# Attention with the values as one high|low tile in two passes, and row sums on GpSimd

## The chip, the cores and the metric

The kernel runs on one core of a Trainium2 chip. The core has a matrix engine (TensorE, PE in the rows; its weight loads are PEld), a vector engine (VectorE, DVE), an activation engine (ScalarE, ACT), GpSimd (POOL) and a queue engine that here only issues transfers (SyncE, SP). They run their own instruction streams and meet at semaphores. The metric is the device time of one execution in microseconds, lower is better.

## The reference

One layer of a hybrid decoder, for a sequence of 2048 tokens of width 1024: a normalised input, one input projection, three token mixers side by side (a recurrent block, forgetting attention, gated linear attention), an output projection and a gated feed-forward. The change is in the forgetting attention, 6 heads of width 64:

```
q = rms_norm(q, q_gain); k = rms_norm(k, k_gain)
cum = cumsum(log_sigmoid(f_logit + b_f))
s = einsum('qd,kd->qk', q, k) * scale + cum[:, None] - cum[None, :]
s = where(k_pos <= q_pos, s, -inf)
p = softmax(s)
o = einsum('qk,kd->qd', p, v)
```

Everything is in 32-bit floats. The kernel gets near that precision by splitting an operand in a high part, rounded to the reduced matmul type (F32R), and a low part, the rest, and adding up the products of the parts.

## The kernel before

The kernel is a row of stages: input projection with the recurrent block, preparation of the attention operands (`fox_operands`), `forgetting_attention`, the gated linear attention, output projection, feed-forward. Each stage is a block with one program for each engine, and stages don't overlap.

`forgetting_attention` makes a loop of 3 passes (`LOOPS`), each over 2 heads. A head has 4 blocks of 512 queries; a block of one head is a unit, 8 units in a pass. A unit is worked off in items: an item is one tile of 128 keys (`kt`) against the unit's 512 queries, so block b has 4(b+1) items and a pass has 80. In the last four items of a unit, the diagonal ones, only 512, 384, 256 and 128 queries are left by the causal mask.

Scores are made twice. `score` makes chunks with queries on partitions (`fa_s_ps`, lines L903 to L906), from which DVE takes row maxima (`maxima`, L850), 22 chunks ahead of their use; `turn_m` and ACT's `copy_m` bring the negated maxima into the operands. `score_t` makes the transposed scores of an item, keys on partitions (`fa_st_ps`, L931 to L934), maxima already subtracted, 3 items ahead (`AHEAD`), in `TB` = 3 PSUM banks: item m+3 takes the bank of item m.

For every item ACT takes the exponential twice, as f32 (`fa_probs`, L822) and rounded (`fa_p_hi`, L823). The residual `fa_p_lo` = `fa_probs` - `fa_p_hi` is made by POOL (L786) for items with kt % 3 = 1, 78 of the 240, and by DVE (L878) for the others. All three have `PB` = 4 buffers, which the value product frees (`pv_done`). PE then makes the value product in three passes (`times_v`):

```
nc.tensor.matmul(o_ps[:, u % 2, qs], v[:, hh, kt, 0:VW], p_hi[:, m % PB, qs], start=first, stop=False, skip_group_check=True)
nc.tensor.matmul(o_ps[0:HEAD_DIM, u % 2, qs], v[:, hh, kt, VW:VW + HEAD_DIM], p_hi[:, m % PB, qs], start=False, stop=False, skip_group_check=True)
nc.tensor.matmul(o_ps[:, u % 2, qs], v[:, hh, kt, 0:VW], p_lo[:, m % PB, qs], start=False, stop=end, skip_group_check=True).then_inc(pv_done, 1)
```

The stationary operand `v[..., 0:VW]` holds the high part of the values in 64 columns and ones in the other 64, so the lower half of `fa_o_ps` is the output and its upper half the row sum. The second pass has the low part of the values, 64 columns.

PE's program is in this order for each item m: score chunk m+22, transposed scores m+3, `turn_m` where one is due, value product m. At the end of a unit its sum is inverted: at kt = 3 of the next unit ACT takes Ln and Exp (`invert`, L815 and L817, each with a table load), DVE waits in `correct` (kt = 2, L865) and makes one Newton step and the scaling in `finish` (kt = 3, L870 and L874); then ACT issues the store. The order of the work is that of the programs; nothing plans it. POOL also copies the values of the next heads into `fa_v` in two pieces (`place_v`, L775 and L776).

Of the kernel before, what the change touches and what calls it, by code (L numbers as in the profile page):

```python
# [14 lines left out]
F32 = mybir.dt.float32  # L15
F32R = mybir.dt.float32r
# [5 lines left out]
P = 128  # L22
# [59 lines left out]
def project_in_and_recur(nc, vec, mod, xT, w_mod, w_in, w_gates, consts, vec_in, proj, mix):  # L82
# [14 lines left out]
    with ExitStack() as ctx:  # L97
        sb = lambda n, s, d=F32: ctx.enter_context(nc.sbuf_tensor(n, s, d))
        ps = lambda n, s, d=F32: ctx.enter_context(nc.psum_tensor(n, s, d))
        sem = lambda n: ctx.enter_context(nc.semaphore(n))  # L100
# [395 lines left out]

def fox_operands(nc, vec, consts, fox_rows, proj, q_split, k_split, bias_split, v_nat):
# [177 lines left out]
def forgetting_attention(nc, consts, q_split, k_split, bias_split, v_nat, mix):  # L675
# [28 lines left out]
    SB, TB, PB = 2, 3, 4  # L704
# [5 lines left out]
    with ExitStack() as ctx:  # L710
# [5 lines left out]
        v = sb("fa_v", [P, HPB, SEQ // P, 3 * HEAD_DIM], F32R)  # L716
# [14 lines left out]
        o_ps, m_ps = ps("fa_o_ps", [P, 2, BLK]), ps("fa_m_ps", [P, BLK])  # L731
# [8 lines left out]
        with nc.Block() as block:  # L740
# [20 lines left out]
            def _(pool):  # L761
# [6 lines left out]
                nc.gpsimd.memset(v[:, :, :, HEAD_DIM:VW].rearrange("p h t n -> p (h t) n").bitcast(F32), 1.0).then_inc(filled, 1)  # L768
                pool.wait_ge(filled, 4)

                def place_v(hh, head, used):

                    pool.wait_ge(pv_done, used)
                    src = v_nat[:, head].rearrange("p o t n -> p (o t) n")
                    nc.gpsimd.tensor_copy(v[:, hh, :, 0:HEAD_DIM], src[:, :, 0:HEAD_DIM].bitcast(F32))  # L775
                    nc.gpsimd.tensor_copy(v[:, hh, :, VW:], src[:, :, HEAD_DIM:].bitcast(F32)).then_inc(v_ready, 1)  # L776

                def lows(base, head):
                    for m, (u, kt, r) in enumerate(ITEMS):
# [4 lines left out]
                        if on_pool(m):  # L784
                            pool.wait_ge(hi_done, base + (m + 1))
                            nc.gpsimd.tensor_tensor(p_lo[:, m % PB, r * P:BLK], probs[:, m % PB, r * P:BLK], p_hi[:, m % PB, r * P:BLK].bitcast(F32),  # L786
                                                    ALU.subtract).then_inc(lo_pool, 1)
                place_v(0, slice(0, 1), NI)
                with pool.Fori(0, LOOPS - 1) as j:
                    lows(NI * j, lambda h: bass.ds(HPB * j + h, 1))  # L790
                last = FOX_HEADS - HPB
                lows(NI * (LOOPS - 1), lambda h: slice(last + h, last + h + 1) if h < HPB else None)

            @block.scalar
            def _(act):
                act.sem_inc(m_copied, 1)
                act.wait_ge(filled, 1)
# [9 lines left out]
                with act.Fori(0, LOOPS) as j:  # L807
# [4 lines left out]
                    def invert(u):  # L812
                        act.wait_ge(pv_done, NI * j + (NI + items_of(u)[-1] + 1))
                        act.wait_ge(fin_done, NU * j + (u + 1))
                        nc.scalar.activation(newton[:, u % 2], o_ps[HEAD_DIM:P, u % 2], ACT.Ln).then_inc(ln_sum, 1)  # L815
                        act.wait_ge(ln_sum, NU * j + (u + 1))
                        nc.scalar.activation(inv_sum[:, u % 2], newton[:, u % 2], ACT.Exp, scale=-1.0).then_inc(inv_done, 1)  # L817
                    for m, (u, kt, r) in enumerate(ITEMS):
                        cols = slice(r * P, BLK)
                        act.wait_ge(st_done, NI * j + (NI + m + 1))  # L820
                        act.wait_ge(pv_done, NI * j + (NI + m + 1 - PB))
                        nc.scalar.activation(probs[:, m % PB, cols], st_ps[:, m % TB, cols], ACT.Exp)  # L822
# [13 lines left out]
            def _(dve):  # L836
# [24 lines left out]
                with dve.Fori(0, LOOPS) as j:  # L861

                    def correct(u):
                        dve.wait_ge(inv_done, NU * j + (u + 1))
                        nc.vector.tensor_tensor(newton[:, u % 2], o_ps[HEAD_DIM:P, u % 2], inv_sum[:, u % 2], ALU.mult).then_inc(corrected, 1)  # L865

                    def finish(u):
                        hh, b = UNITS[u]
                        dve.wait_ge(corrected, 2 * NU * j + (2 * u + 1))
                        nc.vector.scalar_tensor_tensor(out=inv_sum[:, u % 2], in0=newton[:, u % 2], scalar=-2.0, in1=inv_sum[:, u % 2], op0=ALU.add, op1=ALU.mult).then_inc(corrected, 1)  # L870
                        dve.wait_ge(corrected, 2 * NU * j + (2 * u + 2))
# [17 lines left out]
            def _(pe):  # L889
                pe.wait_ge(made, 2)  # L890
                pe.wait_ge(filled, 2)
                pe.sem_inc(st_done, NI)

# [26 lines left out]
                with pe.Fori(0, LOOPS) as j:  # L920
# [16 lines left out]
                    def times_v(m):  # L937
# [17 lines left out]
                    for m in range(NI):  # L955
# [5 lines left out]
                        times_v(m)  # L961
# [775 lines left out]
```

## Time and profile before

| | |
|---|---|
| time, median of 3 runs | 3292.73 us (3290.06 to 3296.04) |
| span of the profiled execution | 3298.2 us |
| PE busy | 2833.0 us, 86% |
| DVE busy | 1457.8 us, 44% |
| ACT busy | 1059.2 us, 32% |
| POOL busy | 900.1 us, 27% |
| attention stage, first score to the start of the next stage | 884 to 1394 us |

No other time is given for the profiled execution than its span; it is 5.5 us above the median of the runs. A busy PE counts overlapping matmuls once and their modelled length, so its share is not its load: the distance between starts is. In a windows row the number behind PE, DVE and so on is its busy time in us, with its instructions in brackets, and the clock is the granted share of full speed. In a timeline row the first number is the start, the second the duration, both in us from the start of the span; what stands in brackets is the idle time of the engine in front of it and what ended that.

### The profile page before, as it was taken

How to read it: one execution, taken by the hardware profiler on the slowest of the kernel's cores; microseconds unless marked ns; L12 is line 12 of the kernel's file. 1: busy time of each engine (PE TensorE's matmuls, PEld its weight loads, DVE VectorE, ACT ScalarE, POOL GpSimd, SP SyncE). 2: the span in 40 equal slices, each digit the busy share in tenths (PEclk: the TensorE clock that was granted, in tenths of full speed). 3: DMA queues.
4: the chain of work that ended last, by engine and by line, in shares of the span. 5: the costliest groups of instructions: out<-in, count | busy, mean ns of one | idle time of the engine just before them, and what ended most of it. 6: DMA issues, size and time to landing. Idle time of an engine off the chain costs nothing. (4 is left out here: it accounts for less than half of the span.)

```text
span 3298.2 us, 34894 instructions
## 1 busy us (share of the span) xinstructions
PE 2833.0 (86%) x12359; PEld 2257.1 (68%) x12359; DVE 1457.8 (44%) x1604; ACT 1059.2 (32%) x1332; POOL 900.1 (27%) x330
## 2 busy tenths in 40 slices
PE   1299999986597979756599699999999999999999
PEld 0177877762275757534487588887888788888887
DVE  5934455525366666555411644314450344214420
ACT  1300134423166666643311233212231222222221
POOL 1301111100121212200132344443444444444343
PEclk9999999996599899956799799999999999999999
DMA  5034333233602020020341422342223322332223
GB/s 218 7 118 169 123 110 93 88 112 105 196 26 66 28 62 0 34 86 13 137 157 76 146 98 92 107 162 96 93 95 132 130 102 88 119 136 90 102 96 102
DMA packets 80770, 330.53 MB, mean 100 GB/s; under 512 B 9239, under 2 KB 10279, under 8 KB 58515
## 3 DMA queue, kind: packets, MB, share of 16 engines
q1 hardware_dynamic: 60368, 280.96, 25.1%
q10 hardware_dynamic: 17984, 39.85, 3.5%
q0 software_dynamic: 2352, 8.93, 0.7%
q8 instruction: 31, 0.51, 0.1%
q14 instruction: 35, 0.28, 0.0%
HBM read 266.69 MB, written 63.01 MB: 100 GB/s over the span
## 5 line engine op out<-in xcount | busy, mean ns | idle before, releaser
L1468 POOL TENSOR_TENSOR ff_w_lo<-ff_w_raw,ff_w_hi 128x2048 fp32r<-128x2048 f32 (+1 forms) x152 | 613.6, 4037 | 879.2 <-ACT ff_w_hi L1497 879.2
L1600 DVE TENSOR_TENSOR ff_a_lo<-ff_gated,ff_a_hi 128x512 f32 x88 | 382.2, 4343 | 148.3 <-ACT ff_a_hi L1507 148.3
L1497 ACT ACTIVATE ff_w_hi<-ff_w_raw 128x2048 fp32r<-128x2048 f32 (+1 forms) x152 | 256.2, 1686 | 356.0 <-PE ff_d_ps L79 356.0
L77 PE MATMUL banks<-h_hi,w_hi 128*128 128x512 f32 x768 | 308.9, 402 | 12.1 <-DVE h_lo L392 12.1
L77 PE MATMUL ff_g_ps<-ff_h_hi,ff_w_hi 128*128 128x512 f32 x704 | 277.5, 394 | 37.8 <-DVE ff_h_lo L1584 31.9
L79 PE MATMUL banks<-h_hi,w_lo 128*128 128x512 f32 x768 | 301.0, 392 | 0.0
L78 PE MATMUL banks<-h_lo,w_hi 128*128 128x512 f32 x768 | 300.9, 392 | 0.0
L78 PE MATMUL ff_g_ps<-ff_h_lo,ff_w_hi 128*128 128x512 f32 x704 | 277.0, 393 | 0.0
L79 PE MATMUL ff_g_ps<-ff_h_hi,ff_w_lo 128*128 128x512 f32 x704 | 276.4, 393 | 0.0
L77 PE MATMUL ff_u_ps<-ff_h_hi,ff_w_hi 128*128 128x512 f32 x704 | 273.9, 389 | 0.0
L78 PE MATMUL ff_u_ps<-ff_h_lo,ff_w_hi 128*128 128x512 f32 x704 | 273.9, 389 | 0.0
L77 PE MATMUL ff_d_ps<-ff_a_hi,ff_w_hi 128*128 128x512 f32 x704 | 273.9, 389 | 0.0
L78 PE MATMUL ff_d_ps<-ff_a_lo,ff_w_hi 128*128 128x512 f32 x704 | 273.9, 389 | 0.0
L79 PE MATMUL ff_d_ps<-ff_a_hi,ff_w_lo 128*128 128x512 f32 x704 | 273.9, 389 | 0.0
L79 PE MATMUL ff_u_ps<-ff_h_hi,ff_w_lo 128*128 128x512 f32 x704 | 273.9, 389 | 0.0
L1503 ACT ACTIVATE ff_silu<-ff_g_ps 128x512 f32<-128x512 f32 x88 | 52.7, 599 | 603.9 <-PE ff_u_ps L79 603.8
L850 DVE TENSOR_REDUCE fa_ch_max<-fa_s_ps 128x1 f32<-128x512 f32 (+2 forms) x262 | 158.9, 607 | 138.3 <-PE fa_s_ps L906 74.9
L1598 DVE TENSOR_TENSOR ff_gated<-ff_silu,ff_u_ps 128x512 f32<-128x512 f32 x88 | 60.5, 688 | 345.8 <-ACT ff_silu L1503 345.8
L786 POOL TENSOR_TENSOR fa_p_lo<-fa_probs,fa_p_hi 128x512 fp32r<-128x512 f32 (+3 forms) x78 | 92.6, 1187 | 404.4 <-ACT fa_p_hi L823 404.4
L1610 DVE SCALAR_TENSOR_TENSOR ff_gated<-ff_d_ps,mod,ff_x_res 128x512 f32<-128x512 f32 x32 | 24.0, 751 | 402.0 <-PE ff_d_ps L79 402.0
L77 PEld LDWEIGHTS ff_g_ps<-ff_h_hi,ff_w_hi 128*128 128x128 f32 x704 | 133.8, 190 | 67.7 <-issue 32.7
L77 PEld LDWEIGHTS banks<-h_hi,w_hi 128*128 128x128 f32 x768 | 145.8, 190 | 45.7 <-DVE h_lo L392 12.5
(253 smaller groups left out, 5208.4 us busy)
## 6 DMA issues: line engine op xcount, KB each, us to landing
ff_w_raw<-in_w_gate_up SPq DMA_DIRECT2D x88, 1024.0 KB, 4.8
ff_w_raw<-in_w_down SPq DMA_DIRECT2D x64, 704.0 KB, 4.0
shared<-in_w_mod SPq DMA_DIRECT2D x24, 1024.0 KB, 6.3
proj_dram<-x_blk SPq DMA_DIRECT2D x96, 256.0 KB, 2.6
w_raw<-in_w_in SPq DMA_DIRECT2D x24, 512.0 KB, 5.1
po_slot<-mix_dram SPq DMA_DIRECT2D x8, 1024.0 KB, 4.8
po_slot<-in_xT SPq DMA_DIRECT2D x8, 1024.0 KB, 4.8
x_dram<-po_slot ACTq DMA_DIRECT2D x8, 1024.0 KB, 3.9
```

What stands on the lines that cost most here:

```text
L77: nc.tensor.matmul(out, hi, act_hi, start=first, stop=False)
L78: nc.tensor.matmul(out, hi, act_lo, start=False, stop=False)
L79: return nc.tensor.matmul(out, lo, act_hi, start=False, stop=last)
L786: nc.gpsimd.tensor_tensor(p_lo[:, m % PB, r * P:BLK], probs[:, m % PB, r * P:BLK], p_hi[:, m % PB, r * P:BLK].bitcast(F32), ALU.subtract). ...
L850: nc.vector.tensor_reduce(ch_max[:, u % 2, i, c:c + 1], s_ps[:, n % SB, 0:w], AX.X, ALU.max).then_inc(max_done, 1)
L1468: nc.gpsimd.tensor_tensor(w_lo[:, s, size(up)], w_raw[:, s, size(up)], w_hi[:, s, size(up)].bitcast(F32), ALU.subtract).then_inc(lo_ready, 1)
L1497: nc.scalar.activation(w_hi[:, s, size(up)], w_raw[:, s, size(up)], ACT.Copy).then_inc(hi_ready, 1)
L1503: nc.scalar.activation(silu[:, s], g_ps[:, s], ACT.Silu).then_inc(silu_ready, 1)
L1598: nc.vector.tensor_tensor(gated[:, s], silu[:, s], u_ps[:, s], ALU.mult).then_inc(gated_ready, 1)
L1600: nc.vector.tensor_tensor(a_lo[:, bass.ds(n, 1)].rearrange("p o n -> p (o n)"), gated[:, s], a_hi[:, bass.ds(n, 1)].rearrange("p o n -> p ...
L1610: nc.vector.scalar_tensor_tensor(out=y_out[:, s], in0=d_ps[:, s], scalar=mod[:, bass.ds(2 * i + (s + GATE2), 1)], in1=x_res[:, s], op0=ALU ...
```

## The change

The stationary operand becomes one tile of 128 columns, high part in 64 and low part in 64, for both passes, over `fa_p_hi` and over `fa_p_lo`. The upper half of `fa_o_ps` is then the product with the low part; DVE copies it out and adds it to the lower half at the end of a unit. The ones are gone from the operand, so the row sums are made elsewhere: for every item POOL adds `fa_probs` into an accumulator `fa_acc` (for kt = 0 it multiplies by a column of ones, which starts the accumulator), and at the end of a unit one f32 matmul with a 128x64 tile of ones adds over the partitions into a new bank, `fa_sum_ps`. ACT now waits also for this addition (`acc_done`) before it writes a buffer of `fa_probs` again. The new bank comes from the transposed scores: `TB` goes from 3 to 2, so item m+3 waits for the exponential of item m+1. The input stage gets a block at its end in which SP clears all of its semaphores (44). The Newton step reads `fa_sum_ps`.

```
@@ project_in_and_recur, behind its block
+        with nc.Block() as block:
+            @block.sync
+            def _(sp):
+                for s in sems:
+                    sp.sem_clear(s)
@@ forgetting_attention
-    SB, TB, PB = 2, 3, 4
+    SB, TB, PB = 2, 2, 4
...
-        v = sb("fa_v", [P, HPB, SEQ // P, 3 * HEAD_DIM], F32R)
+        v = sb("fa_v", [P, HPB, SEQ // P, VW], F32R)
+        acc, ones = sb("fa_acc", [P, 2, BLK]), sb("fa_ones", [P, HEAD_DIM])
...
@@ gpsimd
-                    nc.gpsimd.tensor_copy(v[:, hh, :, 0:HEAD_DIM], src[:, :, 0:HEAD_DIM].bitcast(F32))
-                    nc.gpsimd.tensor_copy(v[:, hh, :, VW:], src[:, :, HEAD_DIM:].bitcast(F32)).then_inc(v_ready, 1)
+                    nc.gpsimd.tensor_copy(v[:, hh], src.bitcast(F32)).then_inc(v_ready, 1)
+                def row_sum(m, base, units):
+                    u, kt, r = ITEMS[m]
+                    pool.wait_ge(hi_done, base + (m + 1))
+                    if kt == 0:
+                        pool.wait_ge(sum_done, units + (u + 1))
+                        nc.gpsimd.tensor_tensor(acc[:, u % 2], probs[:, m % PB], ones[:, 0:1].to_broadcast([P, BLK]), ALU.mult).then_inc(acc_done, 1)
+                    else:
+                        pool.wait_ge(acc_done, base + (m + PB))
+                        nc.gpsimd.tensor_tensor(acc[:, u % 2, r * P:BLK], acc[:, u % 2, r * P:BLK], probs[:, m % PB, r * P:BLK], ALU.add).then_inc(acc_done, 1)
...
+                        row_sum(m, base, units)
@@ scalar
                     def invert(u):
-                        act.wait_ge(pv_done, NI * j + (NI + items_of(u)[-1] + 1))
+                        act.wait_ge(sum_done, NU * j + (u + 3))
...
+                        act.wait_ge(acc_done, NI * j + (m + 1))
                         nc.scalar.activation(probs[:, m % PB, cols], st_ps[:, m % TB, cols], ACT.Exp)
@@ vector, finish
+                        dve.wait_ge(pv_done, NI * j + (NI + items_of(u)[-1] + 1))
+                        dve.wait_ge(corrected, 3 * NU * j + (3 * u + 2))
+                        nc.vector.tensor_copy(newton[:, u % 2], o_ps[HEAD_DIM:P, u % 2]).then_inc(corrected, 1)
+                        dve.wait_ge(corrected, 3 * NU * j + (3 * u + 3))
+                        nc.vector.tensor_tensor(newton[:, u % 2], newton[:, u % 2], o_ps[0:HEAD_DIM, u % 2], ALU.add).then_inc(added, 1)
...
-                        nc.vector.scalar_tensor_tensor(out=o_t[HEAD_DIM * hh:HEAD_DIM * (hh + 1), b], in0=o_ps[0:HEAD_DIM, u % 2], scalar=-1.0, in1=inv_sum[:, u % 2], op0=ALU.mult, op1=ALU.mult).then_inc(fin_done, 1)
+                        nc.vector.scalar_tensor_tensor(out=o_t[HEAD_DIM * hh:HEAD_DIM * (hh + 1), b], in0=newton[:, u % 2], scalar=-1.0, in1=inv_sum[:, u % 2], op0=ALU.mult, op1=ALU.mult).then_inc(fin_done, 1)
@@ tensor
-                        nc.tensor.matmul(o_ps[:, u % 2, qs], v[:, hh, kt, 0:VW], p_hi[:, m % PB, qs], start=first, stop=False, skip_group_check=True)
-                        nc.tensor.matmul(o_ps[0:HEAD_DIM, u % 2, qs], v[:, hh, kt, VW:VW + HEAD_DIM], p_hi[:, m % PB, qs], start=False, stop=False, skip_group_check=True)
-                        nc.tensor.matmul(o_ps[:, u % 2, qs], v[:, hh, kt, 0:VW], p_lo[:, m % PB, qs], start=False, stop=end, skip_group_check=True).then_inc(pv_done, 1)
+                        nc.tensor.matmul(o_ps[:, u % 2, qs], v[:, hh, kt], p_hi[:, m % PB, qs], start=first, stop=False, skip_group_check=True)
+                        nc.tensor.matmul(o_ps[:, u % 2, qs], v[:, hh, kt], p_lo[:, m % PB, qs], start=False, stop=end, skip_group_check=True).then_inc(pv_done, 1)
+                    def row_sums(u):
+                        pe.wait_ge(acc_done, NI * j + (items_of(u)[-1] + 1 + PB))
+                        pe.wait_ge(corrected, 3 * NU * j + 3 * u)
+                        nc.tensor.matmul(sum_ps[0:HEAD_DIM], ones[:], acc[:, u % 2], start=True, stop=True).then_inc(sum_done, 1)
...
                         times_v(m)
+                        if ITEMS[m][0] > 0 and ITEMS[m][1] == 1:
+                            row_sums(ITEMS[m][0] - 1)
+                    row_sums(NU - 1)
```

## Rows read from the trace of the kernel before

**Rows 1.** The page, part 1: busy us, share, instructions.

```profile
PE 2833.0 (86%) x12359; PEld 2257.1 (68%) x12359; DVE 1457.8 (44%) x1604; ACT 1059.2 (32%) x1332; POOL 900.1 (27%) x330
```

**Rows 2.** Windows: item passes, one restart; length, PE, PEld, DVE, ACT, POOL, clock.

```profile
907.00:1057.00 150.00, 135.43 (x653) 107.23 (x654) 99.14 (x177) 106.41 (x198) 35.31 (x30) 0.94 0.11 29
1057.00:1073.00 16.00, 3.70 (x22) 3.10 (x21) 3.83 (x8) 4.29 (x7) 0.00 (x0) 0.64 0.79 198
1073.00:1216.00 143.00, 128.81 (x612) 101.16 (x612) 94.52 (x171) 101.36 (x189) 34.23 (x29) 0.93 0.10 28
...
1234.00:1386.00 152.00, 135.20 (x645) 106.56 (x645) 99.83 (x179) 106.05 (x198) 32.79 (x28) 0.93 0.01 5
```

**Rows 3.** Groups of 884 to 1394 us, shapes apart: busy us, mean ns.

```profile
L878 DVE TENSOR_TENSOR fa_p_lo<-fa_probs,fa_p_hi 128x512 fp32r<-128x512 f32 x114 | 88.7, 778 | 25.6 <-ACT fa_p_hi L823 25.4
...
L950 PE MATMUL fa_o_ps<-fa_p_hi,fa_v 128*64 128x512 f32 x168 | 69.4, 413 | 0.0
...
L786 POOL TENSOR_TENSOR fa_p_lo<-fa_probs,fa_p_hi 128x384 fp32r<-128x384 f32 x12 | 12.1, 1008 | 102.1 <-ACT fa_p_hi L823 102.1
...
L786 POOL TENSOR_TENSOR fa_p_lo<-fa_probs,fa_p_hi 128x256 fp32r<-128x256 f32 x6 | 4.4, 731 | 29.6 <-ACT fa_p_hi L823 29.6
L776 POOL CAST fa_v<-v_nat 128x1024 fp32r x4 | 4.2, 1039 | 0.0
L786 POOL TENSOR_TENSOR fa_p_lo<-fa_probs,fa_p_hi 128x128 fp32r<-128x128 f32 x6 | 2.8, 459 | 9.7 <-ACT fa_p_hi L823 9.7
```

**Rows 4.** Timeline: PE over one item of 512 columns.

```profile
1011.73 0.39 PE L903 MATMUL fa_s_ps<-fa_k_a,fa_q_a 128*128 128x512 f32 x1
...
1012.89 0.40 PE L950 MATMUL fa_o_ps<-fa_p_hi,fa_v 128*64 128x512 f32 x1
1013.12 0.39 PE L951 MATMUL fa_o_ps<-fa_p_lo,fa_v 128*128 128x512 f32 x1
1013.35 0.39 PE L903 MATMUL fa_s_ps<-fa_k_a,fa_q_a 128*128 128x512 f32 x1
```

**Rows 5.** Waits of 907 to 1386 us: total us, times, longest us.

```profile
PE fa_o_ps L949 <- DVE fa_p_lo L878: 40.1, 42, 2.4
```

**Rows 6.** Timeline: ACT between two exponentials at a unit's end.

```profile
1032.66 1.28 ACT L815 ACT_TABLE_LOAD   x1
...
1036.51 0.60 ACT L822 ACTIVATE fa_probs<-fa_st_ps 128x512 f32<-128x512 f32 x1
```

**Rows 7.** Timeline: two residuals that meet, and one of DVE alone.

```profile
934.37 1.29 POOL L786 TENSOR_TENSOR fa_p_lo<-fa_probs,fa_p_hi 128x512 fp32r<-128x512 f32 x1 [4.76 <-ACT fa_p_hi L823]
...
934.64 1.57 DVE L878 TENSOR_TENSOR fa_p_lo<-fa_probs,fa_p_hi 128x512 fp32r<-128x512 f32 x1
...
1000.15 0.68 DVE L878 TENSOR_TENSOR fa_p_lo<-fa_probs,fa_p_hi 128x512 fp32r<-128x512 f32 x1
```

**Rows 8.** Timeline: POOL, DVE and POOL again, in the output projection.

```profile
1612.82 3.44 POOL L1335 TENSOR_TENSOR po_w_lo<-po_w_raw,po_w_hi 128x1024 fp32r<-128x1024 f32 x1 [6.63 <-ACT po_w_hi L1355]
1615.53 2.88 DVE L1380 TENSOR_TENSOR po_m_lo<-po_slot,po_m_hi 128x2048 fp32r<-128x2048 f32 x1 [1.48 <-ACT po_m_hi L1352]
...
1616.52 4.14 POOL L1335 TENSOR_TENSOR po_w_lo<-po_w_raw,po_w_hi 128x1024 fp32r<-128x1024 f32 x1 [0.26 <-ACT po_w_hi L1355]
```

**Rows 9.** Groups of the whole span: plain f32 matmuls; an in-place add on POOL.

```profile
L1341 POOL TENSOR_TENSOR rms_all<-rms_all,po_squares 128x2048 f32<-128x2048 f32 x6 | 27.6, 4602 | 7.3 <-ACT po_squares L1364 7.3
...
L663 PE MATMUL fp_banks<-fp_squares,fp_rows_sel 128*12 128x512 f32 x48 | 20.8, 592 | 1.9 <-ACT fp_squares L577 1.9
```

**Rows 10.** Timeline of the stage before: plain f32 matmuls.

```profile
767.68 7.89 PE L663 MATMUL fp_banks<-fp_squares,fp_rows_sel 128*12 128x512 f32 x18 [1.87 <-ACT fp_squares L577]
```

**Rows 11.** Windows: a stretch of the next stage.

```profile
1564.00:1576.00 12.00, 10.62 (x78) 7.80 (x80) 8.00 (x22) 5.74 (x8) 0.00 (x0) 0.86 0.00 0
```

**Rows 12.** Timeline: SP over a change of stage.

```profile
726.99 0.33 SPq L202 DMA_DIRECT2D proj_dram<-x_blk  x1
...
729.83 0.35 SPq L535 DMA_DIRECT2D fp_ident<-in_consts  x1
```

More of the change, by code:

```diff
@@ L99, in project_in_and_recur, with sem @@
         ps = lambda n, s, d=F32: ctx.enter_context(nc.psum_tensor(n, s, d))
-        sem = lambda n: ctx.enter_context(nc.semaphore(n))
+        sems = []
+        def sem(n):
+            sems.append(ctx.enter_context(nc.semaphore(n)))
+            return sems[-1]
         two = lambda n: [sem(n + "_even"), sem(n + "_odd")]
@@ L730, in forgetting_attention @@
         s_ps, st_ps = ps("fa_s_ps", [P, SB, BLK]), ps("fa_st_ps", [P, TB, BLK])
-        o_ps, m_ps = ps("fa_o_ps", [P, 2, BLK]), ps("fa_m_ps", [P, BLK])
+        o_ps, m_ps, sum_ps = ps("fa_o_ps", [P, 2, BLK]), ps("fa_m_ps", [P, BLK]), ps("fa_sum_ps", [P, BLK])
+        acc_done, sum_done, added = sem("fa_acc_done"), sem("fa_sum_done"), sem("fa_added")
         const_in, made, filled = sem("fa_const_in"), sem("fa_made"), sem("fa_filled")
@@ L767, in _ @@
                 pool.wait_ge(filled, 3)
-                nc.gpsimd.memset(v[:, :, :, HEAD_DIM:VW].rearrange("p h t n -> p (h t) n").bitcast(F32), 1.0).then_inc(filled, 1)
+                nc.gpsimd.memset(ones[:], 1.0).then_inc(filled, 1)
                 pool.wait_ge(filled, 4)
+                pool.sem_inc(acc_done, PB)
                 def place_v(hh, head, used):
@@ L774, in place_v, with lows @@
                     src = v_nat[:, head].rearrange("p o t n -> p (o t) n")
-                    nc.gpsimd.tensor_copy(v[:, hh, :, 0:HEAD_DIM], src[:, :, 0:HEAD_DIM].bitcast(F32))
-                    nc.gpsimd.tensor_copy(v[:, hh, :, VW:], src[:, :, HEAD_DIM:].bitcast(F32)).then_inc(v_ready, 1)
-                def lows(base, head):
+                    nc.gpsimd.tensor_copy(v[:, hh], src.bitcast(F32)).then_inc(v_ready, 1)
[8 more added lines that the diff above has]
+                        nc.gpsimd.tensor_tensor(acc[:, u % 2, r * P:BLK], acc[:, u % 2, r * P:BLK], probs[:, m % PB, r * P:BLK], ALU.add).then_inc(acc_done, 1)
+                def lows(base, units, head):
                     for m, (u, kt, r) in enumerate(ITEMS):
@@ L787, in lows @@
                                                     ALU.subtract).then_inc(lo_pool, 1)
+                        row_sum(m, base, units)
                 place_v(0, slice(0, 1), NI)
                 with pool.Fori(0, LOOPS - 1) as j:
-                    lows(NI * j, lambda h: bass.ds(HPB * j + h, 1))
+                    lows(NI * j, NU * j, lambda h: bass.ds(HPB * j + h, 1))
                 last = FOX_HEADS - HPB
-                lows(NI * (LOOPS - 1), lambda h: slice(last + h, last + h + 1) if h < HPB else None)
+                lows(NI * (LOOPS - 1), NU * (LOOPS - 1), lambda h: slice(last + h, last + h + 1) if h < HPB else None)
             @block.scalar
@@ L796, in _ @@
                 act.sem_inc(m_copied, 1)
-                act.wait_ge(filled, 1)
+                act.wait_ge(filled, 4)
                 for b in range(NBLK):
@@ L812, in invert @@
                     def invert(u):
-                        act.wait_ge(pv_done, NI * j + (NI + items_of(u)[-1] + 1))
+                        act.wait_ge(sum_done, NU * j + (u + 3))
                         act.wait_ge(fin_done, NU * j + (u + 1))
-                        nc.scalar.activation(newton[:, u % 2], o_ps[HEAD_DIM:P, u % 2], ACT.Ln).then_inc(ln_sum, 1)
+                        nc.scalar.activation(newton[:, u % 2], sum_ps[0:HEAD_DIM], ACT.Ln).then_inc(ln_sum, 1)
                         act.wait_ge(ln_sum, NU * j + (u + 1))
@@ L892, in _ @@
                 pe.sem_inc(st_done, NI)
+                pe.sem_inc(sum_done, 2)
                 def score(n, loop):
```

6 lines of the change are left out of this document (3 added, 3 removed).

## The prediction

> **What bounds the kernel now.** I read the page first. TensorE (PE) is busy 86% of the span, GpSimd (POOL) 27%, so over the whole kernel POOL looks free [rows 1]. That share says little here: all of the change but one block of semaphore clears lies in the attention stage, so I read that stage. The windows view gives three passes of 80 items, in stretches of 150, 143 and 152 us (445 us together, 1.85 us an item), with restarts of 16 and 18 us between them; in the first POOL computes nothing and PE little [rows 2]. In the item stretches no engine is full: in the first, PE is "busy" 135 of 150 us by pipelined durations, ACT 106, DVE 99, POOL 35.
>
> What PE really needs is its issue pace. A 512-column matmul follows the one before by 0.23 us, and a whole item, from one L903 to the next, takes 1.62 us when nothing waits [rows 4]. So 512-column items would run at 1.62 us; the rest is waiting. The chain of waits shows the largest item wait of PE: the value products wait for DVE's residual, 40.1 us over 42 waits [rows 5]. Behind that stands ACT: at each of the 24 units it leaves the exponentials for Ln, Exp and two table loads, 3.85 us from the first load to the next exponential [rows 6]. The stage is bound by this cycle (scores, exponential, residual, value product) with PE near its limit between boundaries.
>
> **The change, part by part.**
>
> *Removed pass (L950).* 240 matmuls go. Per unit the diagonal items have 512, 384, 256 and 128 columns, all others 512, so there are 168 of 512 columns and 24 of each other width. By the 0.23 us of [rows 4], scaled by width: 168 x 0.23 + 24 x (0.17 + 0.12 + 0.06) = 47 us of PE. The wider stationary operand costs nothing: the 64-wide L950 and the 128-wide L951 take the same pace [rows 4]. Of L950's row only the count is used; its 413 ns is latency, not pace [rows 3].
>
> *Added row-sum matmul.* 24 matmuls of plain f32, 512 columns. The nearest row is the plain f32 L663, where 18 records take 7.89 us, 0.44 us each; the code has 24 such matmuls and its group 48 records, two a matmul, so 0.87 us [rows 9, 10]. 24 x 0.87 = 21 us. PE nets -26 us. Another engine decides whether any of that is seen.
>
> *Added on POOL.* One two-operand instruction for every item. L786 has the same shape: 1.29 us alone for 512 columns [rows 7], 1.01, 0.73 and 0.46 us for the narrower ones [rows 3]. An in-place add on 2048 columns takes 4.60 us [rows 9], in proportion with some fixed cost, so the add is no cheaper than the subtract. The sums: 168 x 1.29 + 24 x (1.01 + 0.73 + 0.46) = 217 + 53 = 270 us. The residuals that POOL has already: 54 x 1.29 + 12.1 + 4.4 + 2.8 = 89 us. Placing the values costs as before, two casts of 1.04 us or one twice as long, five times: 10 us [rows 3]. POOL alone: 369 us in 445.
>
> *What POOL shares with DVE.* This is the step that decides. At 934.37 POOL starts a 1.29 us subtract and ends at 935.66; DVE starts its residual at 934.64, and instead of the 0.68 us that it takes alone it needs 1.57, ending at 936.21, 0.55 us behind POOL's end [rows 7]. Two SBUF operands on DVE and POOL's two do not run together; the later waits. It works both ways, and in turn: at 1612.82 to 1616.26 POOL runs, DVE (started 1615.53) ends 2.15 us after that, and POOL's next, issued at 1616.52, ends 2.25 us after DVE [rows 8]. So the times add up. DVE's 162 residuals hold the path 0.55 us each at 512 columns: 114 x 0.55 + 48 narrower ones scaled by width, 12.5, = 75 us. In finish, two instructions a unit now have two SBUF operands where one had: 48 x 0.55 = 26 us. Instructions that read PSUM (the maxima) are not in it: none of them is stretched. The shared path needs 369 + 75 + 26 = 470 us, where the items now take 445. For three 512-column items it is 4 x 1.29 + 2 x 0.55 = 6.26 us, 2.09 an item, against PE's new 6 x 0.23 = 1.39. POOL becomes the bound.
>
> The Trainium skill (SBUF — State Buffer, section "Who interferes with whom") says that a DVE instruction with two SBUF inputs contends with a GpSimd instruction that reads SBUF, and that issue order decides who blocks. The trace agrees on the blocking (1.57 against 0.68 us). The page does not promise that a waiting DVE gets its turn between two back-to-back GpSimd instructions; if it did not, the starvation case below would be the result. What rows 8 show is taking turns.
>
> *The boundaries.* POOL idles when it has finished item kt 3 of a unit and exp(kt 4) is not there. Count from POOL's start on the last item of the old unit: its add 0.46, add of kt 0 1.29, residual of kt 1 1.29, perhaps one DVE residual 0.55: PE may multiply kt 1 at 3.1 to 3.6. Then comes the sum matmul: done at 5.0. ACT has issued its table load while waiting, so Ln, load, Exp end at 7.5 (3.85 us less the load, [rows 6]), exp(kt 4) at 8.5. POOL has three more adds and a DVE residual, until 7.6. It idles about 1 us, and about 2.3 before and after the four-item units, whose adds are narrower: 21 inner boundaries, 27 us. Ends: nothing, if sums finish earlier; 3 us each, 63 us, if POOL's backlog is short. The two further DVE instructions in finish (about 0.69 us each by the 0.68 of [rows 7]) push residual kt 5 back 1.4 us; its cover is POOL's three instructions, 3.9 us. Without that cover it is 21 x 1.4 = 29 us, which the upper end holds.
>
> *Two score banks.* The scores of item m+3 now wait for exp(m+1), not exp(m), and behind that wait on PE's queue stands the value product of m. ACT runs ahead of POOL by up to four items, so exp(m+1) is old when PE comes: 0. Where ACT is just back from a boundary the wait is one item's exponentials, about 1 us: 21 us if uncovered.
>
> *Loop ends.* Three times everything waits for the last unit. The sum matmul (0.87) and two DVE instructions (1.4) are new there: 3 x 2.3 = 7 us. The v memset and the ones memset lie under the first loads, 0.
>
> *Clearing the semaphores.* 44 clears on SP and a barrier between stages. No row shows a clear. A stage change without clears takes SP 2.8 us from its last issue to its next [rows 12]; the landing of a transfer is in it. I take 4 us, between 1 (the clears almost free) and 10 (0.2 us each).
>
> *PE's clock.* The item stretches have 0.94 and 0.93, the first restart 0.64 [rows 2], and where PE was busy 10.6 of 12 us in the next stage it is 0.86 [rows 11]. With PE waiting a third of the time I expect near 0.88. At the 1.2 GHz level an item costs PE twice 1.39, 2.8 us, over the shared path's 2.09. I take 8 us, between 0 and 40.
>
> **The sum.** Items 470 + 27 = 497, less 445: +52. Ends +7, clears +4, clock +8: +71. On the profiled span of 3298.2: 3369. The span is 5.5 us above the median of 3292.73, so 3364 on the runs' scale.
>
> **Rivals.**
>
> A, *faster*: the two engines' instructions overlap after all, or back-to-back adds on POOL come cheaper than 1.29 us. Then POOL's 369 us fits in 445 and PE's -26 counts in full, plus 7 + 4 of ends and clears: 3278. It decides where a POOL instruction of 512 columns takes under 1.0 us of the shared path. For it: POOL ran back to back nowhere in this stage, so its price there is unseen. Against: [rows 7, 8, 9].
>
> B, *clearly slower than forecast*: PE falls to 1.2 GHz often and boundaries cost 3 us, or waiting DVE residuals lose their turn to POOL. Upper ends: +36 (boundaries), +29 (finish), +32 (clock), +21 (banks) on 3364 makes 3482; half of that is 3423. For it: POOL's queue is in order, so the residual that PE waits for stands behind two adds. Against: adds and residuals alternate by three.
>
> C, *no change*: the port sum is right but overlaps by the fixed 0.13 us that DVE shows (0.68 against 0.55) on each of POOL's 318 instructions, -41 us, and boundaries vanish, -27. That is 3296.
>
> **Chances.** Forecast (3325 to 3400) 0.67; B 0.17; between C and the forecast 0.05; C 0.03; A 0.08. The range 3312 to 3435 leaves A, C and the tail of B outside. What a measurement here can tell from no change is about 0.2%, 7 us: faster 0.08, same 0.03, slower 0.89.
>
> **What would show it.** POOL's busy share of the item stretches goes from 24% to over 85%; the mean 512-column DVE residual from 0.78 us [rows 3] to 1.2 or more; the largest PE wait becomes the value product on POOL; adds last 1.3 to 1.8 us; item stretches sum to about 500 us; PE's granted clock falls. I am wrong if POOL idles more than 60 us in them (then a chain through ACT and DVE bounds, not the path), if adds take under 1.1 us, or if the clears cost over 10.

## The result, and the profile after

The changed kernel takes 3429.64 us (median of 4 runs, 3422.52 to 3439.96), the kernel before beside it 3291.39 us. The ratio is 1.0417, 95% interval 1.0394 to 1.044: +137 us, where +71 was forecast and 3435 us was the upper end. The sign held, and the time lies 5 us inside the range; the size is nearly twice the forecast.

The page's first part, after. POOL's 302 us more than in [rows 1] are in the main the additions. PE has 192 records fewer and is busy longer all the same:

```profile
PE 2897.1 (84%) x12167; PEld 2284.7 (66%) x12167; DVE 1549.8 (45%) x1652; ACT 1059.9 (31%) x1332; POOL 1201.9 (35%) x564
```

Windows of the three passes and one of the two restarts, columns as in [rows 2]:

```profile
910.00:1102.00 192.00, 157.21 (x583) 116.80 (x583) 125.45 (x188) 106.57 (x199) 132.94 (x105) 0.78 0.08 22
1102.00:1118.00 16.00, 4.51 (x19) 2.83 (x19) 6.09 (x10) 3.18 (x5) 3.15 (x4) 0.73 0.83 210
1118.00:1313.00 195.00, 152.92 (x573) 113.42 (x574) 126.97 (x188) 105.00 (x197) 135.64 (x107) 0.79 0.08 20
...
1330.00:1525.00 195.00, 153.89 (x578) 114.58 (x578) 126.08 (x190) 105.09 (x195) 132.87 (x106) 0.80 0.01 4
```

The passes take 582 us against 445. These 137 us are nearly all of the 140 us by which the two profiled spans differ (3438.1 and 3298.2 us); the restarts are unchanged (16 and 17 us against 16 and 18). POOL is busy 401 of the 582 us, 69%, and so idle 181. PE's granted clock is 0.79 where it was 0.93: between its two levels (2.4 and 1.2 GHz) it spends more of the stage on the lower.

Waits of 884 to 1550 us after: total us, times, longest.

```profile
POOL fa_p_lo L809 <- ACT fa_p_hi L848: 99.6, 38, 6.6
DVE fa_ch_max L875 <- PE fa_s_ps L935: 96.3, 91, 3.9
...
PE fa_st_ps L962 <- ACT fa_p_hi L848: 75.8, 43, 12.0
PE fa_o_ps L980 <- DVE fa_p_lo L908: 64.1, 44, 3.2
...
ACT fa_newton L839 <- PE fa_sum_ps L986: 32.2, 18, 4.2
...
ACT L839 <- PE fa_sum_ps L986: 12.0, 6, 3.2
...
PE fa_o_ps L980 <- POOL fa_p_lo L809: 1.3, 2, 0.9
```

PE hardly waits for POOL at all (1.3 us). It waits for DVE (64.1 us, [rows 5] had 40.1) and, new, for ACT with the scores (75.8 us, of which about 24 are two starts of passes that the kernel before has too). ACT waits for the row sums, 32.2 us in 18 of the 24 units and, before it loads the table, 12.0 us in the other 6. That points to a chain through ACT and DVE, not to a full POOL.

Groups of the stage after, shapes apart, answering to [rows 3]: DVE's 512-column residual went from 778 to 932 ns; the additions take 1485 ns, not 1290.

```profile
L799 POOL TENSOR_TENSOR fa_acc<-fa_acc,fa_probs 128x512 f32<-128x512 f32 x144 | 213.9, 1485 | 33.5 <-ACT fa_p_hi L848 24.9
L908 DVE TENSOR_TENSOR fa_p_lo<-fa_probs,fa_p_hi 128x512 fp32r<-128x512 f32 x114 | 106.3, 932 | 17.5 <-ACT fa_p_hi L848 17.5
...
L904 DVE SCALAR_TENSOR_TENSOR fa_o_t<-fa_newton,fa_inv_sum 64x512 f32<-64x512 f32 x24 | 30.7, 1280 | 1.1
L986 PE MATMUL fa_sum_ps<-fa_acc,fa_ones 128*64 128x512 f32 x48 | 27.9, 666 | 0.1
...
L900 DVE TENSOR_TENSOR fa_newton<-fa_newton,fa_o_ps 64x512 f32<-64x512 f32 x24 | 16.3, 679 | 0.8
```

One boundary of the kernel after, as a timeline (start, duration; compare [rows 6]):

```profile
1023.23 1.28 ACT L839 ACT_TABLE_LOAD   x1
...
1026.63 1.97 PE L986 MATMUL fa_sum_ps<-fa_acc,fa_ones 128*64 128x512 f32 x2
1028.64 0.59 ACT L839 ACTIVATE fa_newton<-fa_sum_ps 64x512 f32<-64x512 f32 x1 [4.13 <-PE fa_sum_ps L986]
...
1029.79 0.69 DVE L875 TENSOR_REDUCE fa_ch_max<-fa_s_ps 128x1 f32<-128x512 f32 x1 [3.88 <-PE fa_s_ps L935]
...
1031.08 0.58 ACT L847 ACTIVATE fa_probs<-fa_st_ps 128x512 f32<-128x512 f32 x1
...
1033.01 1.18 DVE L895 SCALAR_TENSOR_TENSOR fa_inv_sum<-fa_newton,fa_inv_sum 64x512 f32<-64x512 f32 x1
1034.22 0.69 DVE L898 COPY fa_newton<-fa_o_ps 64x512 f32<-64x512 f32 x1
1034.95 0.68 DVE L900 TENSOR_TENSOR fa_newton<-fa_newton,fa_o_ps 64x512 f32<-64x512 f32 x1
1035.66 1.29 DVE L904 SCALAR_TENSOR_TENSOR fa_o_t<-fa_newton,fa_inv_sum 64x512 f32<-64x512 f32 x1
1036.98 0.69 DVE L875 TENSOR_REDUCE fa_ch_max<-fa_s_ps 128x1 f32<-128x512 f32 x1
1037.59 0.77 DVE L908 TENSOR_TENSOR fa_p_lo<-fa_probs,fa_p_hi 128x384 fp32r<-128x384 f32 x1
...
1038.41 0.69 PE L980 MATMUL fa_o_ps<-fa_p_hi,fa_v 128*128 128x384 f32 x1 [3.07 <-DVE fa_p_lo L908]
```

Read it in two halves. First the sum: ACT has loaded its table at 1024.5 and stands for 4.13 us for a matmul that takes 1.97 us at the low clock; it is back at exponentials 7.85 us after the first load (1023.23 to 1031.08), not 3.85. About half of the wait is the matmul's place in PE's queue, behind the product of item 1: it starts at 1026.63. The boundary shown is near the worst, for the longest of these waits is 4.2 us and the mean of the 18 is 1.8. Then the finish: L895 to L904 hold DVE from 1033.01 to 1036.95, behind them a maximum, and only then the next residual. PE, which could have multiplied, stands 3.07 us for it. The clock of the sum matmul stands in the windows view; the second row is a boundary at the full clock, where the same matmul takes 1.07 us (1012.67):

```profile
1026.00:1029.00 3.00, 3.00 (x5) 0.76 (x4) 0.00 (x0) 0.36 (x1) 1.04 (x1) 0.50 0.00 0
1011.00:1014.00 3.00, 3.00 (x12) 1.69 (x11) 2.06 (x6) 1.22 (x2) 2.84 (x5) 1.00 1.01 216
```

So 1.97 us is the matmul at the lower level (0.50), 1.2 GHz.

### The profile page after: what moved, and what is told of

It is laid out like the page before. It is cut to its first block and busy times, and to the rows that moved or that the text cites. A ratio compares the mean times of both kernels' runs of the same rounds, so it can differ in the third digit from the quotient of the medians.

```text
span 3438.1 us, 35360 instructions
## 1 busy us (share of the span) xinstructions
PE 2897.1 (84%) x12167; PEld 2284.7 (66%) x12167; DVE 1549.8 (45%) x1652; ACT 1059.9 (31%) x1332; POOL 1201.9 (35%) x564
## 5 line engine op out<-in xcount | busy, mean ns | idle before, releaser
L77 PE MATMUL banks<-h_hi,w_hi 128*128 128x512 f32 x768 | 309.8, 403 | 10.6 <-DVE h_lo L396 10.6
L77 PE MATMUL ff_g_ps<-ff_h_hi,ff_w_hi 128*128 128x512 f32 x704 | 277.4, 394 | 37.5 <-DVE ff_h_lo L1622 31.7
L799 POOL TENSOR_TENSOR fa_acc<-fa_acc,fa_probs 128x512 f32<-128x512 f32 (+3 forms) x216 | 272.9, 1263 | 57.9 <-ACT fa_p_hi L848 45.5
L226 POOL TENSOR_TENSOR w_lo<-w_raw,w_hi 128x1024 fp32r<-128x1024 f32 x24 | 57.4, 2391 | 353.4 <-ACT w_hi L268 353.3
L962 PE MATMUL fa_st_ps<-fa_q_a,fa_k_a 128*128 128x512 f32 x240 | 114.9, 479 | 75.9 <-ACT fa_p_hi L848 75.8
```

Source lines behind the costliest of these rows:

```text
L77: nc.tensor.matmul(out, hi, act_hi, start=first, stop=False)
L226: nc.gpsimd.tensor_tensor(flat(w_lo[:, s]), w_raw[:], flat(w_hi[:, s]).bitcast(F32), ALU.subtract).then_inc(lo_ready, 1)
L799: nc.gpsimd.tensor_tensor(acc[:, u % 2, r * P:BLK], acc[:, u % 2, r * P:BLK], probs[:, m % PB, r * P:BLK], ALU.add).then_inc(acc_done, 1)
L962: nc.tensor.matmul(out, k_a[:, hh, kts], q_a[:, hh, qs], start=True, stop=False)
```

## The experiments

Times are told as ratios to the kernel before, timed on the same chip, and as that ratio's excess times 3294 us; each ratio is known to about 0.2%, some 6 us. The expectation that was on record stands ahead of each result. Four questions: what do the additions cost, what the banks, what the boundary, and what is the saved pass worth?

**Two banks alone**, in the kernel before:

```
-    SB, TB, PB = 2, 3, 4
+    SB, TB, PB = 2, 2, 4
```

> The kernel before with two banks for the transposed scores and nothing else. Theory 1 (the missing bank is a cost of its own: scores of item m+3 wait for exp(m+1), and behind them the value product; the trace after has 50 us of such waits beside the two loop starts): 15 to 50 us slower, 3305 to 3340. Theory 2 (the shared SBUF path is the whole cost, as the prediction had it): within 7 us of before, 3284 to 3298.

Measured: 3307.98 us, ratio 1.0037 (1.0022 to 1.0052), +12 us, between the two theories. PE's waits of 884 to 1550 us, first one of the kernel before and then two of this one:

```profile
PE fa_st_ps L931 <- ACT fa_p_hi L823: 24.6, 2, 12.3
```

```profile
PE fa_st_ps L931 <- ACT fa_p_hi L823: 73.8, 47, 13.3
...
PE fa_o_ps L949 <- DVE fa_p_lo L878: 8.0, 21, 1.1
```

PE's wait moved: 24.6 us in 2 waits for a score bank became 73.8 in 47, and in return the one for DVE fell from 40.1 to 8.0. The banks are not free, but most of what they cost is a wait that was taken somewhere else before.

**The additions alone**, in the kernel before with its three passes and banks, into an accumulator that nothing reads, with the waits on them and the semaphore clears:

```
...
+                        row_sum(m, base)
...
@@ scalar
+                        act.wait_ge(acc_done, NI * j + (m + 1))
```

> The kernel before, three passes and three banks kept, with GpSimd adding up the exponentials into an accumulator that nobody reads, ACT waiting for it, and the semaphore clears. Theory 1: the adds explain most but not all of +138: 50 to 90 us slower, 3340 to 3380. Theory 2: all of it beyond PE's saving, 140 us or more, 3430 or above. Theory 3 (the adds are hidden, and the new chain at a unit's end costs the time): within 15 us of before.

Measured: 3328.27 us, ratio 1.0095 (1.0078 to 1.0113), +31 us, less than the 50 of theory 1 and more than the 15 of theory 3. About 3 of it are the clears: from SP's last issue of the stage to its next it is 5.6 us here (721.78 to 727.40) and in the kernel after (727.25 to 732.85), where [rows 12] have 2.8. The groups:

```profile
L801 POOL TENSOR_TENSOR fa_acc<-fa_acc,fa_probs 128x512 f32<-128x512 f32 x144 | 218.0, 1514 | 14.8 <-ACT fa_p_hi L850 6.0
L905 DVE TENSOR_TENSOR fa_p_lo<-fa_probs,fa_p_hi 128x512 fp32r<-128x512 f32 x114 | 122.9, 1078 | 24.4 <-ACT fa_p_hi L850 24.3
```

The mutual stretching is real (residual 778 to 1078 ns, more than in the kernel after), and yet all edits of this kernel together cost a quarter of the loss.

**All but the additions**: the kernel after, where only item 0 of each unit goes into the sums, so the output is not the attention. POOL keeps its instruction for item 0 (there an addition of the ones, no multiplication), and for the other items it only raises the semaphore:

```
...
-                        nc.gpsimd.tensor_tensor(acc[:, u % 2, r * P:BLK], acc[:, u % 2, r * P:BLK], probs[:, m % PB, r * P:BLK], ALU.add).then_inc(acc_done, 1)
+                        pool.sem_inc(acc_done, 1)
```

> The kernel after without the adds for kt > 0 (GpSimd only raises the semaphore), so the row sums leave out all keys but the first tile, and a 1 is added to each. All other parts of the change stay. Theory 1: what is left is the PE saving, the missing bank and the longer end of a unit: 3290 to 3330. Theory 2: PE's 26 us come through, about 3275. Theory 3: like after, above 3400.

Measured: 3384.7 us, ratio 1.0269 (1.0248 to 1.029), +89 us, between theory 1 (3330 at most) and theory 3 (above 3400). The additions are worth 48 us on top of the rest, and 89 us are there without them. This is what brings down the forecast's main term: in its waits ACT stands for the sums as before.

```profile
ACT fa_newton L839 <- PE fa_sum_ps L986: 31.1, 18, 4.5
```

**Three banks** in the kernel after, the sum matmul sharing the maxima's bank by partitions:

```
-    SB, TB, PB = 2, 2, 4
+    SB, TB, PB = 2, 3, 4
...
-                        nc.tensor.matmul(sum_ps[0:HEAD_DIM], ones[:], acc[:, u % 2], start=True, stop=True).then_inc(sum_done, 1)
+                        nc.tensor.matmul(m_ps[HEAD_DIM:P], ones[:], acc[:, u % 2], start=True, stop=True).then_inc(sum_done, 1)
```

> The kernel after with three banks for the transposed scores again; the sum matmul writes partitions 64 to 127 of the bank that the turned maxima use, which now take partitions 0 to 3. Theory 1: 20 to 60 us faster than after, 3370 to 3410. Theory 2: the same as after within 10 us, since GpSimd and DVE set the pace on their shared path.

Measured: 3416.83 us, ratio 1.0355 (1.0332 to 1.0379), 20 us less than the kernel after. As above, PE's wait moves back from ACT to DVE's residual (109.0 us in 69 waits).

**The sum matmul early**, on the kernel without the additions:

```
-                        if ITEMS[m][0] > 0 and ITEMS[m][1] == 1:
-                            row_sums(ITEMS[m][0] - 1)
-                    row_sums(NU - 1)
+                        if m == items_of(ITEMS[m][0])[-1]:
+                            row_sums(ITEMS[m][0])
```

> The kernel of e4_no_adds (which took 89 us over the kernel before), with the sum matmul of a unit issued right behind the unit's last value product instead of behind the product of item 1 of the next unit; only item 0 of each unit is in the sums, so the output is not the attention. Theory of the late sum: ScalarE waits for the sums at every boundary (31 us in 18 waits in e4), its exponentials come late, and from there the maxima, TensorE and its clock follow; then this kernel is 20 to 60 us faster than e4, at 3325 to 3365, and ScalarE's wait for the sums is under 5 us. Rival, the long finish: ScalarE's wait goes but VectorE's chain of six steps is as long as before, and the time stays within 10 us of e4, at 3375 to 3395.

Measured: 3354.51 us, ratio 1.0197 (1.0179 to 1.0215), 24 us less than without this edit. ACT's wait for the sums falls from 31.1 us in 18 waits (and 13.0 in 6 before the table load) to 8.6 in 3, not under 5, and PE's for the residual from 43.6 to 21.6 us. The late sum is one part of the boundary.

**The short finish**, on the kernel without the additions: the product with the low values is left out of the output. The last multiplication reads `fa_o_ps` again, as in the kernel before:

```
-                        nc.vector.tensor_copy(newton[:, u % 2], o_ps[HEAD_DIM:P, u % 2]).then_inc(corrected, 1)
-                        dve.wait_ge(corrected, 3 * NU * j + (3 * u + 3))
-                        nc.vector.tensor_tensor(newton[:, u % 2], newton[:, u % 2], o_ps[0:HEAD_DIM, u % 2], ALU.add).then_inc(added, 1)
-                        dve.wait_ge(added, NU * j + (u + 1))
+                        dve.sem_inc(corrected, 1)
...
```

> The kernel of e4_no_adds without the finish's copy out of PSUM and the addition to it, so that the product with the low values is left out of the output (and the sums hold item 0 alone, as there). It takes 2 x 24 VectorE instructions of about 1.2 us away, 57 us of VectorE time, at the boundaries. Theory of the long finish: 30 to 60 us faster than e4, at 3325 to 3355. Rival, the late sum: these instructions stand behind a wait that is there anyway, and the time is 0 to 15 us under e4, at 3370 to 3385. If both sizes come out large, the two stand in one chain and add.

Measured: 3335.73 us, ratio 1.0136 (1.0119 to 1.0153), 44 us less than without this edit: the larger part, though ACT's wait for the sums stays (28.8 us). The last multiplication, 1060 ns in the kernel without the additions, is back at 683 ns, so that 24 x (0.69 + 0.68 + 0.38) = 42 us of DVE are gone (the expectation had put the two instructions at 57):

```profile
L901 DVE SCALAR_TENSOR_TENSOR fa_o_t<-fa_o_ps,fa_inv_sum 64x512 f32<-64x512 f32 x24 | 16.4, 683 | 3.8 <-DVEq L898 1.0
```

**Both together:**

> The kernel of e4_no_adds with both edits of e6_sum_early and e7_short_finish (sums of item 0 alone, product with the low values left out of the output). Each alone gave 30 and 49 us. If they stand one behind the other in one chain, both together give about 79 us, at 3300 to 3315, and what is left over the kernel before is the two banks less the saved pass. If one hides the other, 50 to 60 us, at 3325 to 3335.

Measured: 3324.26 us, ratio 1.01 (1.0082 to 1.0118), 56 us less than without either. By ratios the two alone give 24 and 44, 68 together. They overlap by some 12 us, about what the intervals leave open. The 33 us that stay over the kernel before are more than two banks (12) and the clears (3) make, less the saved pass (12, below). With the banks at the 20 us that they cost in the kernel after, 20 us stay without a name, with 12 it is 30, and they come neither from the additions nor from the longer finish.

**What the third pass is worth**, the kernel before without L950 (the product with the low values is left out):

> The kernel before without its third value pass, so that the product with the low values is left out. That takes 168 of TensorE's matmuls away, about 47 us by their spacing. If TensorE sets the pace of the items in the kernel before, 25 to 47 us faster, at 3245 to 3270. If the chain of exponential, residual and product sets it, less than 15 us, at 3280 or more; then the change had almost nothing to win with its two passes.

Measured: 3279.75 us, ratio 0.9962 (0.9948 to 0.9976): 12.5 us for 47 us of PE. PE's waits of 884 to 1550 us show where most of the other 34 went:

```profile
PE fa_o_ps L949 <- DVE fa_p_lo L878: 62.7, 51, 2.9
```

It was 40.1 us, so 22.6 us of the pass had been done while PE would have waited for the residual. The granted clock is lower as well: 0.89 to 0.91 in the item stretches, against 0.93 and 0.94. In a stage that is otherwise the one before, that is what there was to win with two passes.

**The correction one item later**, in the kernel before:

```
-                        if u > 0 and kt == 2:
-                            correct(u - 1)
                         if u > 0 and kt == 3:
+                            correct(u - 1)
                             finish(u - 1)
```

> The kernel before with VectorE's correction of the reciprocal moved from behind the residual of item 2 to behind that of item 3, so that VectorE isn't held for ScalarE's logarithm and exponential while a residual could be made. If that wait of VectorE for ScalarE (27 us in all in the kernel before by my estimate from one boundary) is on the path, 5 to 20 us faster; if the maxima and residuals behind it are waited for by nobody, within 4 us of the kernel before.

Measured: 3296.7 us, ratio 1.0011 (1.0001 to 1.002). That is within the 4 us of the second theory: DVE's wait for ACT's reciprocal (35.1 us in all in the kernel before) is hidden there, and moving it gains nothing.

**The sum matmul behind item 0**, in the kernel after with all additions:

```
-                        if ITEMS[m][0] > 0 and ITEMS[m][1] == 1:
+                        if ITEMS[m][0] > 0 and ITEMS[m][1] == 0:
```

> The changed kernel with the sum matmul issued behind the value product of item 0 of the next unit instead of item 1. Theory of the late sum (e6_sum_early got 30 us out of it where nearly all additions were left out): ScalarE's wait for the sums, 32 us in 18 waits in the changed kernel, goes, and it is 15 to 35 us faster than the changed kernel, a ratio to the kernel before of 1.031 to 1.037. Rival: with the additions in place TensorE stands at the sum matmul for GpSimd's last addition of the unit, and what ScalarE gains TensorE loses; then less than 8 us, ratio 1.039 to 1.043, and TensorE has a wait for GpSimd's addition of over 15 us in all.

Measured: 3406.91 us, ratio 1.0351 (1.0332 to 1.0369), 22 us less than the kernel after. ACT's wait for the sums falls from 32.2 us in 18 waits to 19.5 in 9 (before the table load from 12.0 to 4.4 in 6), and among PE's waits there is none for an addition.

**The finish spread** over three items, in the kernel after; DVE executes the same instructions:

```
...
+                        if u > 0 and kt == 1:
+                            halve(u - 1)
                         if u > 0 and kt == 2:
-                            correct(u - 1)
+                            join(u - 1)
                         if u > 0 and kt == 3:
+                            correct(u - 1)
                             finish(u - 1)
...
```

`halve` is the copy of the upper half of `fa_o_ps` and `join` the addition to it, into a buffer `fa_whole` of their own.

> The changed kernel with the finish spread: the copy of the product's high half behind the residual of item 1, the addition behind that of item 2, both into a buffer of their own, and the correction and the last two multiplications behind that of item 3. VectorE does exactly as much as in the changed kernel. Theory that the bunch at the boundary costs: 15 to 45 us faster than the changed kernel, ratio 1.028 to 1.037. Rival, that VectorE's additional time itself costs: within 8 us of it, ratio 1.039 to 1.044.

Measured: 3380.32 us, ratio 1.0264 (1.0246 to 1.0282), 50 us less than the kernel after, more than either theory gave it. DVE's time is the same (1553.2 us busy against 1549.8), and only where it lies has changed: added DVE time by itself is not what cost these 50 us. PE's wait for the residual falls from 64.1 to 37.5 us, and DVE's own wait for ACT's reciprocal from 42.3 in 24 waits to 10.6 in 9:

```profile
PE fa_o_ps L990 <- DVE fa_p_lo L913: 37.5, 41, 1.7
```

The groups of `correct`, after and here (the last number is that wait):

```profile
L890 DVE TENSOR_TENSOR fa_newton<-fa_sum_ps,fa_inv_sum 64x512 f32<-64x512 f32 x24 | 16.4, 683 | 42.3 <-ACT fa_inv_sum L841 42.3
```

```profile
L891 DVE TENSOR_TENSOR fa_newton<-fa_sum_ps,fa_inv_sum 64x512 f32<-64x512 f32 x24 | 16.2, 676 | 10.6 <-ACT fa_inv_sum L842 10.6
```

The shorter wait belongs to a change of its own, because this edit also moves `correct` from item 2 to item 3. In the kernel before that move gained nothing; in the kernel after, where the reciprocal comes later, it was not tried alone. How the 50 us divide between the two moves is therefore open. For the bunch itself stands the short finish, which leaves `correct` where it is: 44 us.

**All three**, spread finish, sum behind item 0, three banks:

> The changed kernel with three banks (the kernel of e5_three_banks), the sum matmul behind item 0 and the spread finish, all of the attention computed. If the boundary and the banks are what the change cost beside the additions, most of it comes back: 50 to 80 us faster than the changed kernel, ratio 1.017 to 1.027, the rest being the additions' 31 us and VectorE's longer finish. Rival, GpSimd's queue of additions becomes the bound once the rest is gone: ratio above 1.030 and GpSimd busy over 80% of the item stretches. Under 1.0 only if the saved value pass is worth more than e8_no_third_pass gave (12 us).

Measured: 3363.29 us, ratio 1.0212 (1.0194 to 1.0231), 67 us less than the kernel after, and the fastest here of the kernels with two passes and the whole attention; the kernel before stays faster. Now PE does wait for POOL's residual, 23.8 us, but in the item stretches POOL is busy 397 of 512 us (78%), under the 80% of the rival.

The windows view from the first to the last exponential of the stage, restarts included, columns as in [rows 2]. First before, then after, then the additions alone, no additions, the spread finish, and all three:

```profile
907.00:1386.00 479.00, 410.85 (x1972) 324.36 (x1972) 304.23 (x543) 323.29 (x599) 103.35 (x88) 0.92 0.13 33
```

```profile
910.00:1525.00 615.00, 473.01 (x1772) 350.57 (x1772) 390.80 (x586) 324.27 (x599) 405.85 (x322) 0.79 0.10 26
```

```profile
905.00:1411.00 506.00, 419.06 (x1955) 323.36 (x1954) 359.65 (x539) 323.70 (x598) 400.51 (x325) 0.92 0.12 31
```

```profile
907.00:1466.00 559.00, 431.25 (x1772) 320.99 (x1772) 351.64 (x587) 323.96 (x598) 128.11 (x107) 0.86 0.11 28
```

```profile
907.00:1465.00 558.00, 443.02 (x1765) 327.88 (x1765) 393.49 (x586) 324.11 (x598) 401.73 (x321) 0.84 0.11 28
```

```profile
905.00:1451.00 546.00, 443.62 (x1765) 321.85 (x1764) 390.74 (x585) 322.56 (x598) 406.76 (x321) 0.84 0.11 29
```

Length less PE's busy time is PE's idle time. Before to after it goes from 68 to 142 us, +74, and PE's busy time from 411 to 473, +62, with 200 matmul records fewer. So the loss is half waiting and half a PE that is busy for longer. The row of the additions alone shows what sets it apart: POOL has as much work as after (400.5 us) in a shorter time (83% of the item stretches, 392 of 470 us), yet the clock stays at 0.92 and PE idles 87 us. With the changed boundary and nearly no additions the clock is 0.86 and PE idles 128 us.

## Why the prediction came out as it did

**Right:** the direction; that the saved pass is hardly seen; that the additions take 1.3 to 1.8 us (1485 ns) and stretch DVE's residuals in turn; the clears (4 forecast, SP's interval 2.8 longer); that the restarts barely move (7 forecast); that PE's clock falls (near 0.88 forecast, 0.79 measured). That the time lies in the range is owed to the range's width and not to the mechanism: the forecast's own band was 3325 to 3400 us.

**Wrong by its own test:** POOL's share of the item stretches is 69%, not over 85; it idles 181 us, not under 60; the residual's mean is 932 ns, not 1200; PE's largest waits are for ACT and DVE, not for POOL; the stretches sum to 582 us, not 500. The prediction had named the reading: then a chain through ACT and DVE bounds, not the path.

**The steps, with their sizes:**

- *The shared path as the bound* (470 less 445, +25, and the boundaries' idle POOL, +27): this step failed, since POOL did not become the bound (69% busy; PE waits 1.3 us for it, and 89 of the 137 us are there without the additions). As a size the +25 is close to what the additions alone cost (+31, with the clears); on top of the rest they cost 48 us.
- *"The two further DVE instructions in finish push residual kt 5 back 1.4 us; its cover is POOL's three instructions"*, 0 with 29 as the upper end: this step failed too, and of the boundary's parts it is the largest. The short finish gives back 44 us, the spread one 50, the later correction included. PE does not only wait for POOL's items; the next residual is DVE's own, behind the finish, and at the boundary shown no work of POOL's covers it (PE stands 3.07 us). The finish also grew by more than 1.4 us: L898 and L900 take 1.37 us a unit as forecast, but L904, now with both operands in SBUF, takes 1280 ns for 683, which the prediction had counted on the shared path (0.55 each) and not in this delay. That makes 24 x (1.37 + 0.60) = 47 us of DVE at the one place where everyone waits.
- *ACT at the boundary*, where POOL's idle was put at 1 to 2.3 us: the working had the sum at 5.0 us, with a matmul of 0.87 us at the full clock, and called nothing late but POOL's idle. In the timeline the matmul takes 1.97 us, ACT stands 4.13 us for it and is away 7.85 us. Issuing it earlier gives back 22 to 24 us.
- *Two score banks*, 0 with 21 as the upper end: 12 us in the kernel before, 20 in the one after. The working let ACT run ahead of POOL by up to four items; at the boundary shown it is ACT that is late.
- *PE's clock*, 8 with 40 as the upper end: PE's busy time in the stage rose by 62 us, though its work shrank. An estimate from the rows: 411 less 26 us of work, times 0.92/0.79, makes 448 us, so the clock accounts for the larger part, and some 25 us of the 473 are something else, perhaps matmuls that stand alone and so show their latency. That the clock comes back with the waits is seen in the spread finish (idle 142 to 115 us, clock 0.79 to 0.84, busy 473 to 443 us). How much of it would stay with every wait undone was not isolated.

Taken out of the kernel after one by one, the terms are: additions 48, finish with the later correction 50, late sum 22, banks 20, together 140; with the clears' 3 and less the pass's 12 that is 131 of 137. They are not independent: the last three edits made together give 67, not 92. Rival B, with a chance of 0.17, named these terms (boundaries 36, clock 32, finish 29, banks 21), and half of its sum, 3423 us, is nearer to the measured time than the forecast's 3364. Measured, the finish passed its end, the banks reached theirs, and the late sum came to two thirds of the 36. B's reason was not the one that held, though: it had PE waiting for POOL's residual behind two additions, and PE waits 1.3 us for POOL.

**Open:** of the 70 us that the last version still loses, 31 are the additions and 12 are to be had from the pass, which leaves about 50. Beside it stand 51 us of DVE's longer finish (16.6 + 16.1 + 35.0 - 16.4) and 31 us of PE's sum matmuls; which of them it is was not separated. The kernel with both edits and no additions has the old finish and still 20 to 30 us without a name, so DVE's longer finish cannot be all of it; no run leaves the sum matmuls out.

## What to carry to other kernels

Work that is added at a boundary is not priced by its engine's share but by what stands behind it in that engine's queue: taking 42 us of DVE time out of the bunch gave 44 us, and the same instructions spread over three items, with the correction an item later, gave 50. Before paying for a saved pass, take the pass alone away and time it: 47 us of TensorE were worth 12.5. And check a forecast of a new bound against its rival bottleneck's queue, item by item, not by sums over a stage: POOL's own busy time was forecast at 369 us and came to 401, and even at 83% of the item stretches, with the additions alone, it cost 31 us.

## What the runs showed of the hardware

One operand's place changes a DVE instruction's price under GpSimd load. With both inputs in SBUF the last multiplication takes 1280 ns in the kernel after (L904) and 1434 in the spread version, though the same instruction takes 0.68 us at 1020.49, where POOL starts its next only at 1020.81. With one input in PSUM it takes 683 ns with the additions alone (L901), beside a busy POOL, and the addition of the same shape 679 ns in the kernel after (L900). The Trainium skill (SBUF — State Buffer, section "Who interferes with whom") says that a DVE instruction with at most one SBUF input, outside the modes that use two ports, does not contend with GpSimd; the trace agrees (683 and 679 ns beside additions of 1514 and 1485 ns). Moving an operand from PSUM into SBUF was a cost of this change that came on top of the two new instructions.

The sharing is cheaper in the whole than its single meetings suggest. The prediction added 0.55 us to each 512-column residual of DVE ([rows 7]), from 0.68 to 1.23; with POOL busy 400 of 506 us the mean was 1078 ns, and 932 in the kernel after. DVE's residual gets its turn between additions that follow each other on POOL: from 1022.28 to 1027.04 POOL makes three in a row in the kernel after, and the residual that DVE starts at 1024.92 takes 0.99 us.

A plain f32 matmul of 512 columns (two records) took 1.97 us in the boundary shown and 1.07 in the one before it, against the 0.87 of [rows 9, 10]. The first is at a granted clock of 0.50, the second at 1.00; the second is about one spacing of 0.44 us and one whole record, 592 ns in [rows 9].
